# Four rounded branch tiles in a place of their own, and the shift of two norms moved into the rounding pass

## What is computed

```python
def rms_norm(x, w):
    y = x * lax.rsqrt(jnp.mean(x * x, axis=-1, keepdims=True) + EPS)
    return y * w

def modulate(h, shift, scale):
    return h * (1 + scale) + shift

def merge_branches(h, ret_d, four_d, w_bg, b_bg, w_out):
    gates = jax.nn.sigmoid(h @ w_bg + b_bg)
    g_r, g_f = jnp.split(gates, 2, axis=-1)
    return (g_r * ret_d + g_f * four_d) @ w_out

# first block:  h2 = modulate(rms_norm(x, norm2_w), sh2, sc2);  x = x + g2 * conv_ffn(h2, ...)
# second block: h = modulate_2(rmsnorm(x, norm1_g), sh1, sc1);  proj = h @ w_in
#   merged = g_a * (y_a @ w_proj_a) + g_b * (y_b @ w_proj_b);   x = x + g1 * (merged @ w_out)
```

## Time and profile before

| | |
|---|---|
| median of 3 runs | 2375.86 us |
| the three runs | 2371.9, 2375.86, 2376.02 us |
| the profiled execution | 2371.7 us |
| its span, first to last instruction | 2369.6 us |
| TensorE matmuls busy | 2240.4 us (95%), 10972 |
| VectorE busy | 947.8 us (40%), 1309 |
| ScalarE busy | 614.2 us (26%), 874 |
| GpSimd busy | 143.2 us (6%), 138 |
| DMA | 572.30 MB, mean 242 GB/s |
| mean granted clock of TensorE | 0.98 |

### The profile page before, as it was taken

The page is one execution under the profiler, slowest core; times in us unless marked ns, Lnnn a source line. Parts: engine busy times, 40 slices in busy tenths (PEclk is TensorE's granted clock), DMA queues, the critical chain, the costliest instruction groups (busy, mean ns, idle before and its releaser), DMA issues.

```text
span 2369.6 us, 25330 instructions
## 1 busy us (share of the span) xinstructions
PE 2240.4 (95%) x10972; PEld 1474.5 (62%) x10972; DVE 947.8 (40%) x1309; ACT 614.2 (26%) x874; POOL 143.2 (6%) x138
## 2 busy tenths in 40 slices
PE   7999999999999999999999998999898989899998
PEld 5887788877888888886788884434242434243433
DVE  4848545468888334698724322010101010101011
ACT  5315323343333245336533121000000000000001
POOL 0231000210000011220000110000000000000000
PEclk9999999999999999999999998999999999999999
DMA  7221444435454342320022248999999999999997
GB/s 305 104 77 43 159 160 160 145 144 191 178 213 147 139 142 71 111 75 3 1 71 103 75 164 354 426 431 431 430 431 432 429 431 431 431 430 432 430 428 298
DMA packets 56014, 572.30 MB, mean 242 GB/s; under 512 B 3808, under 2 KB 3936, under 8 KB 36064
## 3 DMA queue, kind: packets, MB, share of 16 engines
q1 hardware_dynamic: 51392, 524.55, 53.7%
q0 software_dynamic: 3216, 29.10, 3.3%
q10 hardware_dynamic: 1296, 17.04, 1.9%
HBM read 568.58 MB, written 2.10 MB: 241 GB/s over the span
## 4 chain that ended last, share of the span: by engine, by line
PE 35%; DMA 17%; DVE 4%; ACT 1%; issue 1%; DVEq 0%; SPq 0%; ACTq 0%
PE ps L1352 10%; PE ps L802 9%; DMA arena<-in_w_exp_up 8%; PE ps L1448 6%; DMA arena<-in_w_exp_gate 4%; DMA weights<-in_w_exp_gate 3%; PE ps L1325 3%; DVE arena L2140 2%; DMA weights<-in_w_exp_down 1%; PE ps L1214 1%; DMA weights<-in_w_exp_up 1%; PE ps L1372 1%; PE ps L1194 1%; PE ps L1160 1%; PE ps L1393 1%
## 5 line engine op out<-in xcount | busy, mean ns | idle before, releaser
L802 PE MATMUL ps<-weights_r 128*128 128x512 f32 (+1 forms) x2784 | 856.0, 387 | 15.5 <-DVE hT_r L2046 7.2
L802 PEld LDWEIGHTS ps<-weights_r 128*128 128x128 f32 x2784 | 521.8, 189 | 129.0 <-issue 14.5
L802 PE MATMUL ps<-hT_r,weights_r 128*128 128x512 f32 x1264 | 462.9, 391 | 0.0
L1352 PE MATMUL ps<-weights,arena 128*64 128x512 f32 x768 | 355.8, 620 | 51.1 <-DMA weights<-in_w_exp_up 37.0
L1354 PE MATMUL ps<-weights,arena 128*64 128x512 f32 x768 | 356.1, 621 | 0.0
L1352 PEld LDWEIGHTS ps<-weights,arena 128*64 128x64 f32 x768 | 106.5, 142 | 287.0 <-issue 249.7
L2027 DVE TENSOR_TENSOR weights_r<-weights,weights_r 128x4096 fp32r<-128x4096 f32 (+1 forms) x45 | 192.6, 4281 | 208.9 <-ACT weights_r L1539 207.1
L802 PEld LDWEIGHTS ps<-hT_r,weights_r 128*128 128x128 f32 x1264 | 238.2, 188 | 49.3 <-issue 0.2
L802 PE MATMUL ps<-arena_r,weights_r 128*128 128x512 f32 (+1 forms) x640 | 225.2, 388 | 0.0
L1539 ACT ACTIVATE weights_r<-weights 128x4096 fp32r<-128x4096 f32 (+1 forms) x46 | 161.6, 3512 | 180.9 <-PE ps L802 115.6
L2689 DVE TENSOR_TENSOR hT<-hT,ps 128x512 f32<-128x512 f32 x32 | 22.0, 688 | 439.4 <-PE ps L1354 439.4
(11 more groups left out here) (319 smaller groups left out, 2403.0 us busy)
## 6 DMA issues: line engine op xcount, KB each, us to landing
weights<-in_w_exp_down SPq DMA_DIRECT2D x21, 4096.0 KB, 31.6
weights<-in_w_exp_gate SPq DMA_DIRECT2D x21, 4096.0 KB, 27.1
weights<-in_w_exp_up SPq DMA_DIRECT2D x21, 4096.0 KB, 28.6
weights<-in_w_in SPq DMA_DIRECT2D x18, 2048.0 KB, 8.0
arena<-in_w_exp_down SPq DMA_DIRECT2D x7, 4096.0 KB, 31.7
arena<-in_w_exp_gate SPq DMA_DIRECT2D x7, 4096.0 KB, 31.2
arena<-in_w_exp_up SPq DMA_DIRECT2D x7, 4096.0 KB, 31.4
weights<-in_w_up SPq DMA_DIRECT2D x11, 2048.0 KB, 8.2
```

What stands on the lines that cost most here:

```text
L802: last = pe.matmul(t, a if w_first else b, b if w_first else a, start=(k == 0 and n == 0), stop=(k == kt - 1 and n == len(pairs) - 1))
L1352: la = pe.matmul(bank(b0 + n)[0:64, :], xe[:, 2 * j + r, 0:64], ra[:, n * 512:(n + 1) * 512], start=start, stop=stop)
```

## The change

Two things are done.

1. `first_highs` gives the first four high halves of branch a a place in `arena`: at 9216 for m1 (where the Fourier mixer's table products `fa` lay before) and at 16384 for m2 (where attention probabilities lay). `branch_high(tag, p, k)` picks the place; TensorE, ScalarE and VectorE use it. ScalarE no longer waits for the last gate tile before the first of them: it makes halves 0 and 1 ahead of its copy-out of tile 1 of gate b 1, and 2 and 3 ahead of that of tile 2.
2. In n2 and n3 the multiply by the column goes into VectorE's multiply (`scalar_tensor_tensor`), ScalarE makes one pass out of two (Identity with the shift as bias, straight into the rounded high half), and VectorE's low half is (value + shift) - high, again a `scalar_tensor_tensor`.

```diff
+        first_highs = {"m1": at(9216, 4, L, rounded=True), "m2": at(16384, 4, L, rounded=True)}
+
+        def branch_high(tag, p, k):
+
+            return first_highs[tag][:, k, :] if p == 0 and k < 4 else (h_high, h_low)[p][:, k, :]
...
+            def norm_shift(m, dst, shift, high):
+
+                for k in range(KT):
+                    act_e.wait_ge(S["scaled"], KT * m + k + 1)
+                    A(high(k, 0, L), dst[:, k, :], ACT.Identity, bias=shift(k)).then_inc(S["h_rounded"], 1)
...
                         for n in range(4):
-                            if i == 3 and n == 3:
-                                wait_full(act_e, (tag, "gate", part, nq, n))
+                            if i == 3 and n == 1:
                                 if tag == "m1":
                                     wait_freed(act_e, ("z", FG - 1))
                                 else:
                                     act_e.wait_ge(S["ya_ready"], NG)
-                                branch_highs(tag, 0, range(1))
+                            if i == 3 and n in (1, 2):
+                                branch_highs(tag, 0, range(2 * n - 2, 2 * n))
...
                     if i == 3:
-                        branch_highs(tag, 0, range(1, branches[tag][0][1]))
+                        branch_highs(tag, 0, range(4, branches[tag][0][1]))
...
-            norm_affine(2, hT, L, lambda k: scale_a[:, 2, k:k + 1], lambda k: mod_cols[:, 24 + k, 0:1],
-                        h_parts[0], 2)
+            norm_shift(2, hT, lambda k: mod_cols[:, 24 + k, 0:1], h_parts[0])
...
-            def low_h(nth, k, high, low, src):
+            def low_h(nth, k, high, low, src, shift=None):
 
                 ve.wait_ge(S["h_rounded"], KT * nth + k + 1)
+                if shift is not None:
+                    ve.scalar_tensor_tensor(low(k, 0, L), src[:, k, :], shift(k), high(k, 0, L).bitcast(F32),
+                                            ALU.add, ALU.subtract).then_inc(S["h_ready"], 1)
+                    return
...
-            norm_scale(2, "n2", xT, hT, L, split_h=(2, *h_parts))
+            ve.wait_ge(S["mods_ready"], 1)
+            norm_scale(2, "n2", xT, hT, L, lambda k: scale_a[:, 2, k:k + 1],
+                       split_h=(2, *h_parts, lambda k: mod_cols[:, 24 + k, 0:1]))
```

More of the change, by code:

```diff
@@ L913, in merge @@
                         p = "ab".index(part)
-                        high, low = (h_high, h_low)[p], branch_lows[tag][p]
-                        x = (lambda k, a, b, v=high: v[:, k, a:b], lambda k, a, b, v=low: v[:, k, a:b])
+                        low = branch_lows[tag][p]
+                        x = (lambda k, a, b, q=p: branch_high(tag, q, k)[:, a:b], lambda k, a, b, v=low: v[:, k, a:b])
                         kt = branches[tag][p][1]
@@ L1583, in branch_highs @@
                 for k in ks:
-                    A((h_high, h_low)[p][:, k, :], branch_views[tag][p][:, k, :], ACT.Copy).then_inc(
+                    A(branch_high(tag, p, k), branch_views[tag][p][:, k, :], ACT.Copy).then_inc(
                         S["branch_high"], 1)
@@ L1832, in _ @@
                 copy_out(("cT2", k), hc2[:, 2 * k:2 * k + 2, :].rearrange("p a b -> p (a b)"))
-            norm_affine(3, hT, L, lambda k: scale_a[:, 0, k:k + 1], lambda k: mod_cols2[:, k, 0:1],
-                        h_parts[0], 3)
+            norm_shift(3, hT, lambda k: mod_cols2[:, k, 0:1], h_parts[0])
             half_high("in2", 1, 0)
@@ L2119, in norm_scale @@
                     if split_h and k >= 2:
-                        low_h(split_h[0], k - 2, *split_h[1:], dst)
+                        low_h(split_h[0], k - 2, *split_h[1:3], dst, split_h[3])
                     if k >= KT:
@@ L2165, in branch_rest @@
                     ve.tensor_tensor(branch_lows[tag][p][:, k, :], branch_views[tag][p][:, k, :],
-                                     (h_high, h_low)[p][:, k, :].bitcast(F32), ALU.subtract).then_inc(
+                                     branch_high(tag, p, k).bitcast(F32), ALU.subtract).then_inc(
                                          S["branch_low"], 1)
@@ L2450, in _ @@
             context(1)
-            norm_scale(3, "n3", xT, hT, L, split_h=(3, *h_parts))
+            ve.wait_ge(S["mods_ready"], 2)
+            norm_scale(3, "n3", xT, hT, L, lambda k: scale_a[:, 0, k:k + 1],
+                       split_h=(3, *h_parts, lambda k: mod_cols2[:, k, 0:1]))
             context(3)
```

2 lines of the change are left out of this document (1 added, 1 removed).

## The result

| | before | after |
|---|---|---|
| median of the runs | 2372.96 us (5 runs) | 2360.77 us (5 runs) |
| lowest to highest | 2371.03 to 2376.02 us | 2355.12 to 2362.54 us |
| the profiled execution | 2371.7 us | 2361.88 us |
| its span | 2369.6 us | 2359.5 us |
| TensorE busy | 2240.4 us, 10972 | 2237.4 us, 10972 |

The kernel is 12.2 us faster by the medians. The ratio is 0.9947, with an interval of 0.9931 to 0.9962, so the gain lies between 9 and 16 us. Of the 8.0 us between forecast and time, 2.9 come from the base (the three runs shown had a median of 2375.86, all five 2372.96), and 5.1 from the gain.

The account below looks back on a forecast made before the run. The prediction took TensorE and its waits to bound the first part, and loads the expert loop. Terms 3.63 + 1.20 + 1.03 + 1.26 = 7.1 us, from the median of 2375.86, gave 2368.8 us, range 2362.5 to 2373.5.

Parts of the forecast that it names:

- the merges' two gaps: First Fourier-branch product and its counterpart in the second merge: TensorE's losses of 1.85 and 1.78 us go, 3.63 us together.
- n2's start: Norm n2: the shorter VectorE and ScalarE chain lets TensorE start 1.20 us earlier.
- the "up" stage: Behind n2: TensorE's waits shrink by 0.33 us at ("up", 2) and 0.7 at ("up", 3), 1.03 us together.
- n3's start: Norm n3: the shorter chain lets TensorE start 1.26 us earlier.
- the clock behind n3: TensorE behind n3: the low-clock stretch moves along with the earlier start, nothing given back.
- Rival D: Merges: their change does nothing because something else ends last; 3.5 us remain, 2372.4 us; chance 0.06.
- Rival C: "up" stage: TensorE stands still longer, n2's gain is lost; 4.9 us remain, 2371.0 us; chance 0.17.
- rival B: Behind n2 and n3: TensorE's low-clock stretches vanish, 3.5 us more, 10.6 in all, 2365.3 us; chance 0.15.
- E: Norms: VectorE's three-operand instructions take 1.69 us each, making the kernel 7.0 us slower, 2382.9 us; chance 0.05.

Follow-up runs that it names:

- the fourteen executions of the table: Profiled executions of the kernel before, the change, its parts alone, and variants with idle products, ScalarE's time put back or the first product held back.
- the kernel before with idle products: Kernel before plus 5 and 3 TensorE products, results unused, ahead of the norms' first products; 2370.10 us against 2372.63, ratio 0.9989.
- the control: The kernel before, unchanged, timed against itself and profiled a third time: 2371.45 us against 2371.74, ratio 1.0001.
- five idle products: The whole change plus 5 and 3 TensorE products, results unused, ahead of n2's and n3's first products; 2359.36 us against 2372.63 for the kernel before, ratio 0.9943.

## Why the prediction was wrong, by its own steps

| term | forecast | in the trace after |
|---|---|---|
| the merges' two gaps | 3.63 | 3.63 |
| n2's start | 1.20 | 1.13 |
| the "up" stage | 1.03 | 0.33 + 1.75 = 2.08 |
| n3's start | 1.26 | 1.43 |
| the clock behind n3 | 0 | 1.51 |
| sum | 7.1 | 9.8 |

The two profiled executions lie 2371.7 - 2361.88 = 9.8 us apart. That the sum meets it to a tenth is luck, since either execution also had pieces of low clock that the other had not: against the change 2.7 us at the beginning and 0.4 us in the spreading products of n2 (1.54 us instead of 1.16), for it some 2.1 us ahead of n3 and 0.9 us between the second attention and the router.

- **The merges**: right, to the hundredth. The rows of the releaser and its cause in ScalarE's program order named the whole wait. Rival D is out.
- **n2**: right. ScalarE's pass with one column took 0.72 us, VectorE's two 0.74 and 0.75, each the value taken from the nearest row. TensorE stood idle for 2.60 us where 2.5 was named.
- **The "up" stage, the first step that failed.** "Bounds 0 and 2.1; I take 0.7, a third, since the w_ada load has a time of its own." The mechanism was right; the term was mis-sized, since the wait shrank by 1.75 of the 2.10 us. The load's delay is not shared out in proportion; in the fourteen executions of the table the load takes either 10.0 to 10.4 us or 8.2 to 8.7. Rival C, which had the stall grow, is out; for the other side the forecast had its bound ("whole or gone, -0.7 to +1.4"), but no rival with a chance.
- **n3**: right; 1.43 for 1.26, and the idle stretch varies by as much from execution to execution (1.32 to 1.55 us in three of the change, 2.75 to 2.93 in three of before).
- **The clock, the second step that failed.** The sum put it at nothing, and rival B, which had it, held 0.15; it gave 1.51 us. What spoke for it in the text, the first merge with full clock behind 1.61 us of idling, was the right row, and the argument against it, that the clock may fall for the tiny products ahead as much as for the idling, was true for n2 alone: there the clock was at 0.50 from 496.00, while the spreading products still ran. It came half: 1.5 of the 3.5 us, behind n3 and not behind n2. The Trainium skill, "TensorE: Matmul & The Clock Gate", Part 1, says that the phase of the clock differs from run to run. The forecast read from it that "the low stretch moves along with the earlier start"; this doesn't hold behind n3, where fourteen executions follow the length of the idle stretch. Ahead of n3 the trace agrees with the page: the same kernel shows 0.86 and 0.72.
- **E**: out. No VectorE instruction of the norms takes longer than 0.75 us on average, as the row of GpSimd's idling said. The rule that the forecast took from the Trainium skill, "SBUF — State Buffer", section "Who interferes with whom", that two-input VectorE instructions and GpSimd's reads of SBUF exclude each other, left the price at zero with GpSimd idle. The trace agrees (GpSimd at 0.00 behind both norms, 16 instructions of 748 ns and 16 of 743 ns):

```profile
L2057 DVE SCALAR_TENSOR_TENSOR hT_r<-hT,mod_cols,weights_r 128x512 fp32r<-128x512 f32 x16 | 12.0, 748 | 1.1 <-ACT weights_r L1534 0.8
L2140 DVE SCALAR_TENSOR_TENSOR hT<-xT,scale_a,ps 128x512 f32<-128x512 f32 x16 | 11.7, 743 | 2.4 <-PE ps L886 2.4
...
L1534 ACT ACTIVATE weights_r<-hT,mod_cols 128x512 fp32r<-128x512 f32 x16 | 11.4, 722 | 10.5 <-DVE hT L2140 10.5
```

- **The range.** With a sum of 9.8 the forecast would have been 2366.1 from the base of 2375.86, and 2363.2 from that of the five runs, 2372.96; both lie inside. The time fell out below because three things added up, each about 2 to 3 us: the two terms, a base from three runs that was 2.9 us high in a kernel whose single executions lie between 2363.17 and 2377.92 us, and the 2.4 us of the next paragraph. The range reached 6.3 us below the forecast: room for any two of the three, not for all.

**What stays open.** Between the 9.8 us of the terms and the 12.2 of the medians lie 2.4 us, inside the interval of the ratio (9 to 16). The mean clock rose by about 0.002, of which the stretch behind n3, about 0.43 of 4 us in 2360, is 0.0007; by the 1.35 us per 0.001 estimated above, the other 0.0013 would be some 1.8 us, most of the 2.4. Every variant shows a part of the rest, even the kernel before with idle products, whose clock behind the norms did not change. Where in the program it comes from, no comparison of single traces can say, since the control differs from its own twin by 4.5 us, and why the clock is higher stays open.

## What to carry to other kernels

An operation taken off an engine that nobody waits for is not free of effect: follow it to the slot it frees and to the load that this releases, and ask which other transfer that load collides with; here such a collision was there or not there in fourteen executions, and a third of it is a value that none shows. Where an idle stretch is shortened, look up the granted clock behind stretches of the new length elsewhere in the same trace, and give that row the weight. But look first whether the clock falls behind the stretch, as at n3, or has fallen with the small work ahead of it, as at n2: a shorter stretch gives it back only in the first case. And take the base from many runs before arguing about the last three microseconds.

## What the hardware showed that was not expected

- The granted clock behind TensorE's idling is reproducible at n3: 1.00 in the seven executions with 0.95 to 1.74 us of idling, 0.57 to 0.68 in the seven with 2.11 to 3.06 us. The price is 1.3 to 1.7 us each time, on top of the idling itself. In the seven low ones the clock was at 1.00 late in the idle stretch, and fell between 0.5 us ahead of the first product and 1.4 us behind it.
- Behind n2, with its long row of small products in front, the clock was low with 1.83, 2.60, 3.73 and 3.92 us of idling, and full with 0.45 us after five idle products. The length of the idling does not decide there: in the change the clock stood at 0.50 from 496.00 on, ahead of the idle stretch, and with the idle products it was back at 1.00 before the first product began.
- The load of w_ada took 10.0 to 10.4 us with the load of w_up issued 4.4 to 5.0 us ahead of it, and 8.2 to 8.7 us with 5.7 to 8.2 us between them (six and eight executions).
- The same kernel's clock falls in different places from execution to execution, which moves single stretches by 3 us (365.22 or 368.32 between the second attention and the router), and the mean clocks of those two executions, 0.981 and 0.980, hardly show it.
